# Seven products for eight in the gate and up projections of the second block's feed-forward

## What is computed

```python
def rmsnorm(x, g):
    xf = x.astype(jnp.float32)
    y = xf * lax.rsqrt(jnp.mean(xf * xf, axis=-1, keepdims=True) + RMS_EPS)
    return (y * g.astype(jnp.float32)).astype(x.dtype)

def swiglu(h, w_gate, w_up, w_down):
    return (jax.nn.silu(h @ w_gate) * (h @ w_up)) @ w_down
...
        h = rmsnorm(x, ffn_pre_g[layer])
        x = x + rmsnorm(swiglu(h, ffn_w_gate[layer], ffn_w_up[layer], ffn_w_down[layer]), ffn_post_g[layer])
```

## Time and profile before

| | us |
|---|---|
| median of 3 runs | 2394.31 (2393.95 to 2394.52) |
| the profiled execution | 2391.58 |
| its span, first to last instruction | 2389.8 |
| TensorE busy | 2341.5 (98%) |
| TensorE, weight loads | 1929.5 (81%) |
| VectorE busy | 1347.5 (56%) |
| GpSimd busy | 1229.2 (51%) |
| ScalarE busy | 1047.3 (44%) |

### The profile page before, as it was taken

One profiled execution on the slowest core, in us unless ns is written; L12 is line 12 of the kernel. 1 busy time (PEld: TensorE's weight loads), 2 busy tenths in 40 slices (PEclk: granted clock), 3 DMA queues, 4 the chain that ended last, 5 costly groups with the idle time before them and its releaser, 6 DMA issues.

```text
span 2389.8 us, 32547 instructions
## 1 busy us (share of the span) xinstructions
PE 2341.5 (98%) x12840; PEld 1929.5 (81%) x12840; DVE 1347.5 (56%) x2210; ACT 1047.3 (44%) x1654; POOL 1229.2 (51%) x915
## 2 busy tenths in 40 slices
PE   8999999999999999999999999999999999999997
PEld 6777688989877767898988769888889779888887
DVE  4687587675548866867665446322225768322224
ACT  5345573444343456553444455322224485322223
POOL 4435277786543253787783453554454334554442
PEclk9999999999999999999999999999999999999999
DMA  5213123232322131233232212322332312322331
GB/s 187 75 62 107 36 88 106 91 105 89 106 89 71 56 113 54 88 107 106 89 123 88 85 36 62 115 88 88 106 106 89 106 53 80 115 89 88 105 106 36
DMA packets 153975, 214.58 MB, mean 90 GB/s; under 512 B 7776, under 2 KB 94944, under 8 KB 153568
## 3 DMA queue, kind: packets, MB, share of 16 engines
q1 hardware_dynamic: 153824, 212.51, 27.3%
HBM read 208.30 MB, written 2.10 MB: 88 GB/s over the span
## 4 chain that ended last, share of the span: by engine, by line
PE 86%; DVE 5%; ACT 4%; POOL 3%; issue 2%; SPq 0%; DMA 0%; ACTq 0%; DVEq 0%; POOLq 0%
PE ps L452 64%; PE ps L485 13%; POOL w_lo L414 2%; PE ps L1024 2%; PE ps L1005 2%; PE ps L1047 1%; PE ps L2185 1%; PE ps L1499 1%; DVE h_lo L748 1%; DVE x L871 1%; DVE tmp_both L866 1%; PE ps L1537 1%; ACT w_hi L353 0%; PE ps L1546 0%; ACT L672 0%
## 5 line engine op out<-in xcount | busy, mean ns | idle before, releaser
L414 POOL TENSOR_TENSOR w_lo<-raw,w_hi 128x512 fp32r<-128x512 f32 (+1 forms) x648 | 859.6, 1365 | 982.4 <-ACT w_hi L353 977.1
L452 PE MATMUL ps<-h_hi,w_hi 128*128 128x512 f32 (+1 forms) x1248 | 507.4, 407 | 10.5 <-POOL w_lo L414 10.4
L452 PE MATMUL ps<-h_hi,w_lo 128*128 128x512 f32 (+1 forms) x1248 | 487.4, 391 | 0.0
L452 PE MATMUL ps<-h_lo,w_hi 128*128 128x512 f32 (+1 forms) x1248 | 487.2, 390 | 0.0
L452 PE MATMUL ps<-hid_hi,w_hi 128*128 128x512 f32 x928 | 366.9, 395 | 10.3 <-POOL w_lo L414 4.8
L452 PE MATMUL ps<-hid_hi,w_lo 128*128 128x512 f32 x928 | 361.5, 390 | 0.0
L452 PE MATMUL ps<-hid_lo,w_hi 128*128 128x512 f32 x928 | 361.4, 389 | 0.0
L353 ACT ACTIVATE w_hi<-raw 128x2048 fp32r<-128x2048 f32 (+2 forms) x145 | 246.3, 1724 | 172.9 <-PE ps L452 110.8
L452 PEld LDWEIGHTS ps<-h_hi,w_hi 128*128 128x128 f32 (+1 forms) x1248 | 234.5, 188 | 72.4 <-issue 18.0
L452 PEld LDWEIGHTS ps<-h_hi,w_lo 128*128 128x128 f32 (+1 forms) x1248 | 233.8, 187 | 51.5 <-issue 0.2
L452 PEld LDWEIGHTS ps<-h_lo,w_hi 128*128 128x128 f32 (+1 forms) x1248 | 234.3, 188 | 50.7 <-issue 5.5
(11 more groups left out here) (355 smaller groups left out, 4524.6 us busy)
## 6 DMA issues: line engine op xcount, KB each, us to landing
raw<-in_w_down SPq DMA_DIRECT2D x32, 1024.0 KB, 4.9
raw_u<-in_w_up SPq DMA_DIRECT2D x28, 1024.0 KB, 5.2
raw<-in_ffn_w_gate SPq DMA_DIRECT2D x44, 512.0 KB, 3.8
raw<-in_ffn_w_up SPq DMA_DIRECT2D x44, 512.0 KB, 4.7
raw<-in_w_in SPq DMA_DIRECT2D x20, 1024.0 KB, 5.0
raw<-in_ffn_w_down SPq DMA_DIRECT2D x20, 1024.0 KB, 4.9
raw<-in_w_out SPq DMA_DIRECT2D x8, 1024.0 KB, 6.4
raw<-in_ev_w_in SPq DMA_DIRECT2D x8, 1024.0 KB, 5.1
```

Of the source, the lines that this page charges most:

```text
L414: pool.tensor_tensor(slot.lo(k)[:, 0:slot.width], raw[r][:, k, 0:slot.width], slot.hi(k)[:, 0:slot.width].bitcast(F32), ALU.subtract).then ...
L452: mm = pe.matmul(o, lh, rh, start=first and q == 0, stop=last and q == 2, skip_group_check=True)
```

## The change

In both layers of the second block, groups up[2] to up[10] become quarter groups of two slots. A slot now holds 128 gate and 128 up channels, from two loads in rows of 512 bytes. up[0] and up[1] stay plain. The units lie in seven cells instead of eight (free stretches, two idle tables, and the token half of `h_hi` and `h_lo` that no product reads any more after up[1]); so unit k of a slot takes the cell of unit k of the slot before. The down projections are cut into halves: each quarter group from up[4] on has one half (four rows, one set of four banks) ahead of it, for hidden channels two groups back, and all downs use one half of PSUM, all quarter groups the other. VectorE makes the silu's inputs and products out of the joined quadrants (`strassen`), and the eight `hf` blocks, the t differences and their parts are made at the start of the stage.

```diff
+        def quarter_tiles(pe, g, n_u, t_ready, t_hi=t_hi, t_lo=t_lo):
...
+            pl.up, pl.down = [up(CH2 * 512, first), up(0, 1 - first)], []
+            pl.down.append([down(CH2 * 512, REST2 // P, n, (first + n) % 2) for n in range(2)])
+            pl.up.append(gated_quarters(256, first))
+            pl.up.append(gated_quarters(512, 1 - first))
+            for n in range(4, UPS):
+                c, e = divmod(n - 4, 2)
+                if e == 0:
+                    pl.down.append([])
+                pl.down[-1].append(down(512 * c, KT, e, first))
+                pl.up.append(gated_quarters(256 * (n - 1), 1 - first))
+            pl.down[-1].append(down(512 * (CH2 - 2), KT, 1, first))
...
+                for e in range(2):
+                    rest(tiles_of(pl.down[0][e], FEAT, hid_hi, hid_lo, ready=("hid_lo_done", lo0)))
+                quarter_tiles(pe, pl.up[2], 0, "t_done", t_hi2, t_lo2)
+                quarter_tiles(pe, pl.up[3], 2, None, t_hi2, t_lo2)
+
+                def down(c, e):
+                    pe.wait_ge(*at("hid_lo_done", 4 * c + 6))
+                    rest(tiles_of(pl.down[1 + c][e], FEAT, hid_hi, hid_lo, k0=KT * (1 - c % 2)))
+
+                for n in range(4, UPS):
+                    down(*divmod(n - 4, 2))
+                    quarter_tiles(pe, pl.up[n], 2 * (n - 2), None, t_hi2, t_lo2)
+                down(CH2 - 2, 1)
+                pe.wait_ge(*at("hid_lo_done", 2 * UPS))
+                to_next.tensor(pe, 2, None, KT)
...
+                for n in range(2, UPS):
+                    nx = u_slot(n + 1) if n + 1 < UPS else None
+                    ub = u_slot(n) + 1
+                    units_hi(act, ub, 0, 1)
+                    p1_copy(n, 0)
+                    units_hi(act, ub, 1, 7)
+                    if n >= 3:
+                        stream_hi(act, ub + 2)
+                    p1_copy(n, 1)
...
+                def join(n, i):
+                    t, u = slice(256 * i, 256 * i + 256), 2 * (n - 2) + i
+                    dve.wait_ge(*at("p1_copied", u + 1))
+                    dve.wait_ge(sems["unit_used"], st.slots[u_slot(n) + i].unit0 + 3)
+                    link(dve, dve.tensor_tensor(u_p16[:, i, :], u_p1[:, i, :], bank(n, 3)[:, t], ALU.add))
+                    sg["p5_added"].by(dve.tensor_tensor(u_q[0][:, i, :], u_p16[:, i, :], bank(n, 1)[:, t], ALU.add))
+                    dve.wait_ge(*at("p5_added", u + 1))
...
+                def strassen(n):
+                    ub, nx = u_slot(n) + 1, u_slot(n + 1) if n + 1 < UPS else None
+                    units_sum(dve, ub, 0, 1)
+                    join(n, 0)
+                    units_sum(dve, ub, 1, 2)
+                    join_more(n, 0)
+                    units_sum(dve, ub, 2, 4)
+                    join(n, 1)
...
+                for n in range(2, UPS):
+                    if n >= 4:
+                        down(1 + (n - 4) // 2, n % 2)
+                    strassen(n)
+                down(CH2 - 1, 1)
```

202 lines of the change are left out of this document (144 added, 58 removed).

## The result

| | before | changed |
|---|---|---|
| median of 4 runs, us | 2394.13 (2392.93 to 2394.52) | 2412.62 (2411.34 to 2413.10) |
| ratio, 95% interval | | 1.0077 (1.006 to 1.0095) |
| profiled execution, us; its span | 2391.58; 2389.8 | 2412.42; 2410.6 |

What follows compares the result with a forecast made beforehand. TensorE's matmul time was taken as the bound. Per layer 7.4 + 1.4 + 9.3 + 7.7 = 25.8 us lost against 15.7 gained, 10.1 net, 20.2 in all, gave a forecast of 2414 us, range 2385 to 2436.

Steps and rivals of the forecast that it cites:

- What bounds, and the gain: Second block's feed-forward stage: TensorE's matmul time bounds; quarter groups save 1.74 us each, 15.7 us a layer.
- A: Start of the stage, once a layer: down[0] waits for its weights, 5.8 us net, plus 1.6 of half clock: 7.4 us.
- B: First Strassen group, started by TensorE at T: VectorE reaches its join late, about T + 7.8; 1.4 us lost with the next.
- C: Second Strassen group, directly behind the first: VectorE and GpSimd taking turns delay its join to T + 35.6; 9.3 us lost.
- D: Seven later groups: GpSimd's fourth weight row for each down half comes 1.1 us late, 7.7 us a layer.
- E: End of the stage: the closing pair's weights are in time; nothing lost.
- Loads: Quarter loads in 512 B rows: 9.4 us at twice the packets, slot free 12 us before use; nothing lost.
- Sum: All terms: 25.8 us lost against 15.7 gained, 10.1 us a layer, 20.2 in all; forecast 2414 us.
- The faster: Rival: VectorE and GpSimd rarely meet, only the start's loss stays, 8.3 us a layer gained; 2378 us, chance 0.18.
- the even case: Rival: half the turns between VectorE and GpSimd are missed; 2388 to 2396 us, chance 0.10.
- The much slower case: Rival: the join is late in every period, VectorE's 33 us becoming the period; 2442 us, chance 0.07.
- the sum of 1.95: Rival: a VectorE and GpSimd pair of turns takes 1.26 + 0.69 us, not 1.72; some 2427 us, chance 0.03.

Runs made afterwards that it cites:

- a_start: Changed kernel with, at each stage's start, ScalarE's hf blocks ahead of rstd's exponentials, t_total earlier and down[0]'s upper weights ahead of t_high: 2407.94 us.
- b_start: a_start with VectorE's order changed too: two of four t_lo and the last two weight sums behind the evacuation of up[1]'s banks; 2408.55 us.
- b2_start: a_start's edits with VectorE's start pieces ordered by when each is asked for, the products of up[1] last; 2408.73 us.
- x3: Changed kernel with b2_start's, d_late's and c_tail's orders, up[1]'s low parts and down[0]'s second evacuation behind the first join, four end rows split later: 2383.69 us.
- c_tail: Changed kernel with the first Strassen group's two hid_lo behind the second group's first join, and ScalarE's two hid_hi later: 2410.05 us.
- n_prod: Changed kernel with five VectorE products per Strassen group made on 8 of 512 columns (work left out, outputs wrong): 2396.91 us.
- d_cells: Changed kernel with unit weights going round eleven cells instead of seven and all down projections sharing one buffer: 2412.32 us.
- d_late: Changed kernel with TensorE's products in the halves from down[1] on reordered, asking for the fourth row 4.1 us in, not 2.0: 2402.03 us.

## Why the prediction was right, and where it was not

The time came out 1.4 us under the forecast, but errors of opposite sign lie under that, so the closeness is luck; the mechanism, VectorE and GpSimd in each other's way behind a start that ScalarE's order delays, is not.

- **What bounds, and the gain.** A Strassen group is 20.07 us in each later period, half a down 10.9: 9 x 1.69 = 15.2 us a layer for 15.7. Right.
- **A, 7.4 us.** Measured 6.4 of wait and 12.55 for down[0] at a clock of 0.87, against 11.41 before with its wait: 19.11 - 11.41 = 7.7 (8.1 in the second layer). Size and chain right, in the order named: hf, up[0], t_hi, weights. Incomplete was the reading of it: "the second half of down[0] needs up[1]'s banks, which VectorE reaches ... about 1534; TensorE reaches them at 1533 to 1535, so nothing more" was the sign that VectorE is just as late, and it should have been read as a second bound at the same place. a_start, b_start and b2_start showed it: 1.6 to 2.0 us of the 7.7 come back for ScalarE's order and VectorE's, the rest only with work moved into VectorE's idle time further on (x3: 10.1 us of start and groups together, c_tail's 3.7 among them).
- **B, 1.4 us.** Nothing: 20.08 us. VectorE's eight copies were done at T + 2.9, and its join came at T + 4.6 to T + 5.4, not at T + 7.8.
- **C, 9.3 us.** 28.58 - 20.07 = 8.5 us. Right in place and cause. In size two errors meet: the join ended at T + 34.1, not T + 35.6, and TensorE's waits come to 7.0 us from start to start; the other 1.5 us are the half clock behind them (granted 0.94), which the prediction priced in A alone. The rows in turn at 1.67 to 1.78 us are those of the earlier trace rows. c_tail takes 3.7 us of it by order, n_prod 3.6 by leaving work out.
- **D, 7.7 us.** 5.6 us (5.5 in the second layer): 1.55 once, 0.8 five times, and none in the seventh half. The working's own moments, T + 23.05 against T + 22.1, give 0.95 us, and not the 1.1 that was summed. The place (fourth row) was right. The fourth row was done at T + 22.8 (1688.3 for the group of 1665.5), not T + 23.05, and in the last half there is no next group whose sums GpSimd could meet. The first cause that it named, the seven cells, is there (0.58 us) but does not decide (d_cells); the order in which TensorE asks is the lever (d_late).
- **E, "nothing".** Wrong, 5.3 us in the first layer. The working stopped at the pair's own weights, which are in time as it says. It left out the eight rows of the next layer behind them, which before ended ahead of ssum and now lie over it. What is split later still has to be split, and falls on someone. The earlier trace rows would have given a part of the price: where the engines took turns ssum took 1.36 us and the stretch was 31.1 us, 1.5 over before. The 5.07 us it does not give.
- **Loads.** Right, 3.7 and 4.8 us.
- **Sum.** B, C and D came 1.4, 0.8 and 2.1 us a layer below their terms, A 0.3 to 0.7 above, the gain 0.5 below, and small excesses add 0.4: 7.1 to 7.3 lost a layer instead of 10.1; E's 5.3 and 1.2 us ahead of the stage made up for it: 20.9 for 20.2 between the profiled executions. Neither was forecast. With a closing stretch as in b_start and the clock ahead of the stage as before, the time would be some 5 us lower, about 2408 (an estimate from these rows).
- **Rivals.** The faster and the even case needed turns that are missed; the second group's rows show none missed. The much slower case needed a late join in every period; from the third group on there is no wait for it. Its own sum was off as well: 33 over 31.9 is 1.1 us a group and not 2, and so some 2429, not 2442. The Trainium skill (SBUF — State Buffer, section "SBUF: two separate sides") has the shared pair as a lock that the one that starts first holds for its whole instruction. n_prod agrees in kind: operations of 8 columns ended only with the row of GpSimd that was running. In size it does not: a pair of turns was again 1.72 us, not the sum of 1.95. Stretch E goes beyond it: VectorE's operation waited not for one instruction of GpSimd but until four or five of them were through.

What stays open: what decides whether GpSimd passes the turn on after each row (C, D, d_cells) or not for four or five (E in six of the thirteen profiled executions with the changed stage, 5.07 to 5.48 us; a seventh, n_prod, with 3.30, where GpSimd's run was over after three rows; d_late's second group). No experiment set it on or off by itself. The moment at which ssum comes does not decide it alone: it began 0.50 us into a row of GpSimd in a_start (5.11 us) and 0.49 us into one in c_tail (1.36 us). That the scatter between runs of one kernel is this long sum is not shown. It fits that the profiled executions of b2_start and c_tail, without it, are the fastest of their five, and those of a_start and d_late, with it, the slowest; but x3's slowest is without it, and there the clock was half for 6.8 us more in the first block.

## What to carry to other kernels

A wait names the instruction that came last, not the engine that is full: before reordering for it, take each engine's busy share of the stretch around it; where one is as full as VectorE was at the start here (18.62 of 19.11 us), reordering within the stretch only moves the wait, and work must leave it or go into that engine's idle time behind. Read a busy share with care: it counts the time that an operation waits for its turn (5.07 us for a sum of 0.68). When VectorE and GpSimd both have SBUF work, count VectorE's operations in turns of GpSimd's rows, not in columns alone. Price the half clock behind each long wait, not only behind the first. When a change makes weights come later, follow them past their own use, to what they now lie over; and before adding cells for a row that is late, ask for it later.
